# VectorE turns the expert rows, two more weight places in the second layer, and 16 KB pieces for the first layer's down weights, in a four-stage diffusion trunk on one core

## What is computed

```python
def hier_moe(x, w_group, b_group, w_router, b_router, w_gate, w_up, w_down):
    ...            # top-1 of 4 groups, then top-2 of its 4 experts, weights in `combine`
    y = jnp.zeros_like(x)
    for e in range(MOE_EXPERTS):                       # 16
        hdn = jax.nn.silu(x @ w_gate[e]) * (x @ w_up[e])     # 1024 -> 512
        y = y + combine[:, e:e + 1] * (hdn @ w_down[e])      # 512 -> 1024
    return y
```

## Time and profile before

| | us |
|---|---|
| time, three runs | 1120.63, 1123.94, 1128.57 |
| median | 1123.94 |
| profiled execution: time / its span | 1123.72 / 1121.9 |
| TensorE busy | 1031.8 (92%) |
| VectorE / ScalarE / GpSimd busy | 378.0 / 200.9 / 90.0 |
| granted TensorE clock, mean | 0.964 |

### The profile page before, as it was taken

The page is one execution under the profiler, slowest core; times in us unless marked ns, Lnnn a source line. Parts: engine busy times, 40 slices in busy tenths (PEclk is TensorE's granted clock), DMA queues, the critical chain, the costliest instruction groups (busy, mean ns, idle before and its releaser), DMA issues.

```text
span 1121.9 us, 20021 instructions
## 1 busy us (share of the span) xinstructions
PE 1031.8 (92%) x8395; PEld 623.4 (56%) x8395; DVE 378.0 (34%) x785; ACT 200.9 (18%) x383; POOL 90.0 (8%) x134
## 2 busy tenths in 40 slices
PE   2899999999997999999999976996897999998896
PEld 1343433448445788888888863543544655544442
DVE  1100799547546411111111104546516311111112
ACT  2200022325214200000000013314503100000001
POOL 4200000000100200000000014000010100000000
PEclk9799999998998999999999997997998899999998
DMA  9999868670021499999999994542022699999993
GB/s 341 397 394 387 316 218 293 249 299 2 4 76 75 141 397 393 419 388 384 411 381 405 415 370 128 214 150 75 1 78 113 252 407 413 398 400 399 416 427 143
DMA packets 71189, 313.31 MB, mean 279 GB/s; under 512 B 6280, under 2 KB 7912, under 8 KB 60641
## 3 DMA queue, kind: packets, MB, share of 16 engines
q1 hardware_dynamic: 58656, 283.64, 65.0%
q0 software_dynamic: 7168, 16.33, 4.4%
q10 hardware_dynamic: 5312, 12.59, 2.9%
HBM read 303.81 MB, written 15.20 MB: 284 GB/s over the span
## 4 chain that ended last, share of the span: by engine, by line
PE 78%; DMA 12%; DVE 5%; issue 2%; ACT 1%; SPq 1%; ACTq 0%; PEldq 0%; POOL 0%; POOLq 0%; DVEq 0%
PE ps L511 52%; PE ps L942 10%; DMA ring<-in_moe_w_gate 9%; PE ps L524 4%; PE ps L833 2%; PE ps L969 2%; DMA ring<-in_ada_w 2%; PE ps L931 2%; PE ps L1036 1%; SPq L450 1%; PE ps L767 1%; PE ps L955 1%; PE ps L1206 1%; DMA y_rows<-ar 1%; ACT hT L1295 0%
## 5 line engine op out<-in xcount | busy, mean ns | idle before, releaser
L511 PE MATMUL ps<-ring,ar 128*32 128x384 f32 (+5 forms) x3992 | 508.7, 471 | 16.6 <-DMA ring<-in_moe_w_gate 7.6
L511 PEld LDWEIGHTS ps<-ring,ar 128*32 128x32 f32 (+2 forms) x3992 | 216.7, 121 | 151.5 <-issue 84.1
L942 PE MATMUL ps<-ring,ar 128*32 128x128 f32 x1632 | 185.4, 274 | 0.0
L942 PEld LDWEIGHTS ps<-ring,ar 128*32 128x32 f32 x1632 | 177.6, 111 | 0.4
L511 PE MATMUL ps<-hT,ring 128*128 128x512 f32 x256 | 114.3, 601 | 0.1
L511 PE MATMUL ps<-ring,hT 128*128 128x512 f32 x192 | 87.1, 611 | 1.6 <-ACT hT L1295 1.6
L511 PEld LDWEIGHTS ps<-hT,ring 128*128 128x128 f32 x256 | 48.2, 192 | 64.2 <-issue 63.7
L2074 DVE SCALAR_TENSOR_TENSOR ar<-ar,cpar 128x512 f32<-128x512 f32 x120 | 79.6, 741 | 0.0
L1956 DVE COPY ar<-ps 128x384 f32<-128x384 f32 (+1 forms) x33 | 16.3, 493 | 181.5 <-PE ps L955 94.2
L524 PE MATMUL ps<-ring,silu_c 128*32 128x512 f32 x384 | 51.3, 655 | 22.0 <-DMA ring<-in_ada_w 22.0
L511 PEld LDWEIGHTS ps<-ring,hT 128*128 128x128 f32 x192 | 36.8, 195 | 49.7 <-issue 47.8
(11 more groups left out here) (321 smaller groups left out, 885.3 us busy)
## 6 DMA issues: line engine op xcount, KB each, us to landing
ring<-in_moe_w_gate SPq DMA_DIRECT2D x33, 2048.0 KB, 19.3
ring<-in_moe_w_up SPq DMA_DIRECT2D x33, 2048.0 KB, 18.8
ring<-in_moe_w_down SPq DMA_DIRECT2D x33, 2048.0 KB, 20.4
ring<-in_ada_w SPq DMA_DIRECT2D x24, 2048.0 KB, 13.5
ring<-in_even_w_in SPq DMA_DIRECT2D x5, 2048.0 KB, 18.9
ring<-in_odd_w_in SPq DMA_DIRECT2D x3, 2048.0 KB, 23.8
y_rows<-mla POOLq DMA_DIRECT2D x12, 384.0 KB, 11.4
y_rows<-ar ACTq DMA_DIRECT2D x16, 288.0 KB, 8.4
```

Source lines behind the costliest of these rows:

```text
L511: return nc.tensor.matmul(o, l, r, start=start, stop=stop)
L942: m = nc.tensor.matmul(ps[96:128, bank, g * P:(g + 1) * P], xgT[:, p, c, 32 * g:32 * g + 32], w[:, c, 3 * P:HID], start=c == 0 and g == 0, ...
```

## The change

Four things are changed together.

1. **Rows are turned by DVE.** `do_xt`, `do_hidden_t` and the copies from PSUM behind them go. DVE turns blocks of 32 by 32 elements from `xg` to `xgT` (`do_rows_turned`: 12 instructions of 32 partitions by 256 elements in layer 0, 8 in layer 1) and from `hid` to `hidT` (`do_hidden_t`: 16 instructions, of 96 elements in layer 0 and of 64 in layer 1). Only the first tile of each layer still goes through TensorE.
2. **Down weights of layer 0 in 16 KB pieces.** They are now loaded as in layer 1, row 4p+c. The hidden units must then stand in another order, so the gate and up products of layer 0 read their weight columns with a step: three of every four for the 384-column matmuls, and every fourth one (16 bytes apart) for the 128-column matmuls.
3. **Two more places in layer 1.** `x` and `hT` become one tensor `xh`, `gb` and `mla` one tensor `gm`, and two blocks of 16 KB per partition are cut from them (`beside`). Gate 15 and up 15 (`BESIDE`) are loaded there, before down 0; down 14 and down 15 take their places in `ring`.
4. **`final_norm_g`** goes to `gb[:, 0]` and is loaded after layer 1's gathers were issued, since its old place is one of the new weight places.

```diff
+BESIDE = (("g", 1, NEXP - 1), ("u", 1, NEXP - 1))
...
+    for n, (b, down) in enumerate(zip(BESIDE, (("d", 1, NEXP - 2), ("d", 1, NEXP - 1)))):
+        places[at[down]], turns[at[down]] = places[at[b]], turns[at[b]]
+        places[at[b]], turns[at[b]] = SLOTS + n, 2
...
             def expert_src(kind, l, e):
-                if kind == "d" and l == 0:
-                    return A["moe_w_down"][l, e, :, :].rearrange("(c p) n -> p c n", c=HC)
                 if kind == "d":
                     return A["moe_w_down"][l, e, :, :].rearrange("(p c) n -> p (c n)", c=HC)
...
+                    if l == 1 and b == ("d", 1, 0):
+                        for n, w in enumerate(BESIDE):
+                            if n == 0:
+                                sp.wait_ge(sem("block_used"), at["oin", 0, 1] + 1)
+                            else:
+                                sp.wait_ge(sem("q_rot"), 2)
+                            sp.dma_start(flat(at[w]), expert_src(*w)).then_inc(arrival(at[w]), 16)
+                    load(at[b], expert_src(*b), wide=flat(at[b]))
...
+                    wv = w[:, c, :].rearrange("p (i k) -> p i k", k=4)
                     if l == 0:
                         for g in range(3):
                             m = mm(ps[32 * g:32 * g + 32, bank, 0:3 * P], xgT[:, p, c, 32 * g:32 * g + 32],
-                                   w[:, c, 0:3 * P], c == 0, c == KC - 1)
+                                   wv[:, :, 0:3], c == 0, c == KC - 1)
                         for g in range(3):
                             m = nc.tensor.matmul(ps[96:128, bank, g * P:(g + 1) * P], xgT[:, p, c, 32 * g:32 * g + 32],
-                                                 w[:, c, 3 * P:HID], start=c == 0 and g == 0,
+                                                 wv[:, :, 3], start=c == 0 and g == 0,
...
+            def do_rows_turned(l, p):
+                for g in range(CAP[l] // 32):
+                    slots = slice(32 * g, 32 * g + 32)
+                    for q in range(4):
+                        m = V.transpose(xgT[32 * q:32 * q + 32, p, :, slots],
+                                        xg[slots, p, :].rearrange("s (c q i) -> s q c i", c=KC, q=4)[:, q, :, :])
+                return m
+
+            def do_hidden_t(l, p):
+                for r in range(4):
+                    cols = hid[32 * r:32 * r + 32, p, 0:hid_width(l)]\
+                        .rearrange("s (g q i) -> s q g i" if l == 0 and r == 3 else "s (q i c) -> s q c i", i=32, q=4)
+                    for q in range(4):
+                        m = V.transpose(hidT[32 * q:32 * q + 32, p, 0:3 - l, 32 * r:32 * r + 32], cols[:, q, :, :])
+                return m
...
                 def step(e, p, last=False):
                     hidden_t(l, e - 1, 1 - p)
                     if l == 1:
                         mix_weights(e - 1, 1 - p)
+                    if not last:
+                        rows_turned(l, e + 1, 1 - p)
                     hidden(l, e, p)
-                    if l == 0 and not last:
-                        xgt_half(e + 1, 1 - p)
                     y_half(l, e - 1, 1 - p)
...
             gathers(1)
+            pool.wait_ge(sem("x_added"), 2 * NT + 2 * NLAT)
+            pool.dma_start(gb[:, 0, :], A["final_norm_g"].rearrange("(a n) -> a n", a=1).to_broadcast([P, D]))\
+                .then_inc(sem("small_in"), 16)
             overflow(1)
```

More of the change, by code:

```diff
@@ L133, in ring_places @@
     after = range(len(freed), len(freed) + 3)
-    return [slot[b] for b in freed] + [k % SLOTS for k in after], [nth[b] for b in freed]
+    places, turns = [slot[b] for b in freed] + [k % SLOTS for k in after], [nth[b] for b in freed]
+    at = {b: k for k, b in enumerate(freed)}
+    for n, (b, down) in enumerate(zip(BESIDE, (("d", 1, NEXP - 2), ("d", 1, NEXP - 1)))):
+        places[at[down]], turns[at[down]] = places[at[b]], turns[at[b]]
+        places[at[b]], turns[at[b]] = SLOTS + n, 2
+    return places, turns
 def hybrid_dit(nc, A, out):
@@ L474, in moe_stream @@
                         overflow_stream(0)
-                    load(i, expert_src(kind, l, extra if e == LAST else e), wide=expert_dst(kind, l, SLOT[i]))
+                    k = at[BESIDE[e - NEXP + 2]] if l == 1 and kind == "d" and e >= NEXP - 2 else i
+                    load(i, expert_src(kind, l, extra if e == LAST else e), k, wide=flat(i))
             def overflow_stream(l):
@@ L604, in logits @@
                     m = nc.tensor.matmul(ps[32 * g:32 * g + 32, 0, j * P:(j + 1) * P], w_rt[:, 32 * c:32 * c + 32],
[L605 removed]
+                                         h_tail(l)[:, c, j * P:(j + 1) * P], start=c < 4, stop=c >= 4, skip_group_check=True)
                 m.then_inc(sem("logits_ps"), 1)
@@ L922, in rows_and_router @@
                     pe.wait_ge(sem("idx_ready"), 2)
-            def do_xt(l, p):
-                n = CAP[l]
-                for c in range(KC):
-                    bank, o = (3 + c // 4, (c % 4) * n) if l == 0 else (2, c * n)
-                    m = nc.tensor.transpose(ps[:, bank, o:o + n], xg[0:n, p, c * P:(c + 1) * P], ident[0:n, 0:n])
-                return m
             def do_product(l, p, up, w):
@@ L949, in do_product @@
                                wv[:, :, 2 * g:2 * g + 2], c == 0, c == KC - 1)
-                return m
-            def do_hidden_t(l, p):
-                if l == 0:
-                    for c in range(3):
-                        m = nc.tensor.transpose(ps[:, 2, c * P:(c + 1) * P], hid[:, p, c * P:(c + 1) * P], ident)
-                else:
-                    for c in range(2):
-                        m = nc.tensor.transpose(ps[:, 2, c * P:(c + 1) * P], hid[:, p, c:256:2], ident)
                 return m
@@ L1085, in experts, with step @@
                     key_spread()
-                def step(e, p, i, t, last=False):
+                def step(e, p, i, t):
                     gate_up(l, e, p, i, t, False)
@@ L1092, in step @@
                         mix_in(e - 2, p)
-                    hidden_t(l, e - 1, 1 - p)
                     gate_up(l, e, p, i + 1, t, True)
-                    if not last:
-                        xt(l, e + 1, 1 - p)
                     down(l, e - 1, 1 - p, i + 2, t)
@@ L1366, in experts, with step @@
             def experts(l):
-                xgt_half(l, 0, 0)
+                first_xgt(l)
                 silu(l, 0, 0)
-                xgt_half(l, 1, 1)
                 if l == 0:
                     last_taken()
-                def step(e, p, last=False):
+                def step(e, p):
                     silu(l, e, p)
-                    if not last:
-                        xgt_half(l, e + 1, 1 - p)
                     if l == 0:
@@ L1384, in experts @@
                 n = act.value_load(ov_n, min_val=0, max_val=MAXOV)
-                step(NEXP - 1, 1, last=l == 1)
+                step(NEXP - 1, 1)
                 overflow(l, n)
                 if l == 0:
-                    step(LAST, 0, last=True)
+                    step(LAST, 0)
                     A_(rstd[:, 15:16], eps, ACT.Sqrt)
@@ L2309, in gather @@
                     pool.wait_ge(sem("idx_ready"), 2)
-                if not (isinstance(e, int) and e < 2 and l == 0):
-                    pool.wait_ge(sem("xgT_ps"), EB[l] + e - 1)
+                if not (isinstance(e, int) and e < 2):
+                    pool.wait_ge(sem("xgT_dve"), EB[l] + e - 1 - l)
                 ex = e if isinstance(e, int) else bass.ds(e, 1)
```

162 lines of the change are left out of this document (74 added, 88 removed).

## The result

The changed kernel takes **1320.6 us** (median of 4 runs, 1310.7 to 1322.0) against 1122.6 us before (4 runs, 1120.6 to 1128.6): a ratio of 1.170, interval 1.166 to 1.175. It was forecast at 1117. The profiled execution spans 1318.8 us (1121.9 before). The clock is not the cause: over the span it was granted at 0.959 of full speed, and at 0.99 from 460 to 860 us.

A forecast was written before the change was run, and what follows sets the result against it. Layer 0 was taken as bound by TensorE, with weight loads nearly as slow, layer 1 by the DMA engines. Layer 0's 7.7 + 2.4 - 2 = 8.1 us less layer 1's 1.4 gave 6.7 us faster, 1117.0 us, range 1107 to 1127.

The forecast's parts named there:

- stepped columns: Rival: layer 0's fourth column group, reading every fourth element, slows gate and up 1.47 times; 59 us slower, 1183; chance 0.10.
- Turning on TensorE, layer 0: Layer 0: 1.29 us per expert leave TensorE, the stage becomes bound by the DMA engines; 7.7 us gained.
- the stock: Layer 0: weights loaded ahead of TensorE, run down to 5.9 us at gate 15; that much was to be gained.
- the pieces: Layer 0's down weights in 16 KB pieces: 0.15 us for each of 16 blocks, 2.4 us gained (0 to 21).
- list of signs: Expected profile: layer 0 periods 17.2 us at the start, some 17.7 from about the sixth expert, with waits for weights.
- The hand-over: From layer 0's end to layer 1: expert 15's store and the gather compete with more loads; 2 us lost (0 to 5.8).
- DVE: Both layers: transposes on DVE take 0.2 us each, hidden behind other work; cost nothing except in layer 1's tail.
- Two more places: Layer 1: they free TensorE only behind down 13's landing; 0.3 us gained, a loss of 3.3 at 0.425 per transpose.
- `final_norm_g` and the tail: Layer 1: 512 KB move into the bound stream, 1.7 us lost; with 0.3 gained by the places, 1.4 us later.
- Sum: Layer 0 8.1 us earlier, layer 1 1.4 later: 6.7 us faster than 1123.72, giving 1117.0 us.
- the gain is lost at the hand-over and in the tail: Rival: store and gather 5.8 us dearer, pieces worth nothing, transposes 0.4 us: 1127, or half, about 1121; chance 0.20.

The follow-up runs named there:

- d_step4_alone: The kernel before with one edit: the fourth column group reads every fourth column, transposes and pieces as before; 1330.1 us (one run).
- f_steps: The kernel before, with the fourth column group's 128 columns read in another step or pattern in each of 8 K steps; 1215.8 us (one run).
- a_dense16: The changed kernel with layer 0's gate and up on dense columns again, hidden rows turned by 12 VectorE instructions, not 16; 1126.1 us, ratio 1.0011.
- i_places_early: a_dense16 with the two more places holding layer 1's gate 2 and up 2 instead of gate 15 and up 15; 1122.4 us, ratio 0.9964.

## Why the prediction was wrong, step by step

**The step that failed is the price of the stepped columns.** The prediction named the rival with its mechanism and its point of decision (slower than before from a factor of 1.12 on), and then gave it a chance of 0.10 and a factor of 1.47, from weight loads at step two. Both were off. The factor is 2.2 (0.238 us per pass against 0.107), as d_step4_alone and f_steps show, and gate and up grew by 12.6 us per expert where 5.0 were priced. The argument against it was wrong in kind: "each fp32 column takes about 1.7 ns, a pace at which one element need not be slow to fetch". The pace of a pass is 0.83 ns per column (0.107 us over 128); a line of 16 bytes costs 1.9 ns (0.238 us over 128). The 1.7 was two passes taken as one: the row cited has 16 records for the 8 products of a down block, so it gives 0.89 ns per column and pass. The claim that one element need not be slow to fetch had no row behind it. The other fact held against it, that layer 1 reads two of four at almost full speed, was true (the row is gate 15's, not an up block's, with the same shape) and said nothing of one in four: two elements per line are the last cheap case (287 ns a record at step 2, 352 at step 3, 413 at step 4).

**What would have been the right weight.** The prediction itself said that one of four is in no row, and the nearest row it had, 206 ns against 140, pointed the right way, as the 413 ns against 279 now show. A term with no row of its own, on the engine that bounds the stage, multiplied by 17 experts, should not have had a chance of 0.10.

**Turning on TensorE, layer 0.** Judged by a_dense16. The stage does become bound by the DMA engines: TensorE waits there for up, gate and down blocks, 8.0 + 1.4 + 0.8 = 10.2 us in all, where it waited for none. At the hidden product of expert 15 a_dense16 is 8.7 us ahead (632.6 against 641.3 us, with first gate products 0.01 us apart); the forecast was 5.9 for the stock and 2.4 for the pieces. That is right, and so is the mechanism: the loads of gate blocks 3 to 15 landed 17.5 us apart (410.9 and 620.7), where 17.7 was forecast and 17.85 was before. The period at the start was 15.7 us (the loads of 393.68 and 409.36), as the prediction's own 15.9 said and not the 17.2 of its list of signs, and it held for eight experts, not five. What the prediction didn't follow is the expert in place 16. TensorE comes to its gate product 9.7 us ahead (642.57 against 652.26). Inside that product it stands still for 2.8 us, with the block landed at 637.2 and no releaser in the trace, and its granted clock is 0.53 from 641 to 652 us, against 0.84 from 651 to 662 before. At hidden product 16 5.1 us are left, and after the 5.1 us wait for VectorE 1.2 at down 16 (670.2 against 671.4). Why TensorE stands still there is not shown.

**The hand-over.** Forecast 2 us lost. The loads that follow the gathered rows are issued 4.3 us sooner (692.56 against 696.88 us), 0.8 less than the 5.1 at the result of down 15. Layer 1's first gate product keeps 2.9 (871.1 against 874.0). Forecast 8.1, so most of the miss without the stepped columns is here and in place 16.

**DVE.** Mis-sized: the turnings take 0.435 us (32 x 256), 0.39 to 0.41 (32 x 128), 0.29 (32 x 96) and 0.24 (32 x 64), not 0.2. VectorE's 17 us per expert were enough cover inside the stages, as forecast; at their ends there is none, and there the size counts, twice.

**Two more places.** Right in kind: down 13 starts 211.9 us behind layer 1's first gate product in a_dense16 and 212.7 before, and from it to the end 36.2 us against 35.2. So 0.8 is gained ahead of down 13 and 1.0 lost behind it, where the forecast was 0.3 gained there, and 3.3 lost at the dear end of a turning. i_places_early shows the reason given for it, that the places stand behind the last point at which the DMA engines bind: used early they are worth 5 to 8 us of layer 1 in the traces.

**`final_norm_g` and the tail.** Layer 1 with its end: forecast 1.4 us later, measured 0.2 (248.1 against 247.9), less than one execution can resolve. The row's own price, 1.7, was not measured alone.

**Sum.** Without the stepped columns the forecast was 6.7 us gained. The trace of a_dense16 has 2.7; its median lies between 2.4 us faster and 4.8 slower than before. So of the rest the rival "the gain is lost at the hand-over and in the tail" came nearest, with layer 0's last expert and the hand-over as its places and not layer 1's tail.

## What to carry to other kernels

A layout that makes one operand cheaper to load or to turn may be paid for by whoever reads it with a step, here with 12.6 us per expert: price the moving operand of TensorE first, per 16-byte line and not per element, and take 1.9 ns per line against 0.83 ns per fp32 column and pass, as worked out here from the K steps and from f_steps. Two fp32 elements of each line, read in order, cost little (an estimated 121 ns a pass against 109), and so do three of four (a record of 384 columns 501 ns against 490); one of each line more than doubled the pass (0.238 us against 0.107). Where turnings move to an engine with slack, look at the last round of each stage, where nothing covers them, and at what waits in front of them in that engine's queue; a buffer gained is worth what it brings forward in the bound queue, so the first blocks may repay it (5 to 8 us of layer 1 in single traces here) where the last did not.

## What the runs showed of the hardware that I had not expected

- TensorE's moving operand, fp32: in f_steps' rows but that of step 16 the pass is, by estimate and within 6 ns, the longer of 0.83 ns per column and 1.9 ns per 16-byte line read. Step 2 287 ns a record, step 3 352, steps 4, 5, 8 and 16 391 to 413, dense 273 to 279.
- Alignment alone did it: pairs inside a line 286 ns, the same pairs across a border 418.
- Two runs read in turn cost 304 ns, 31 above the cheapest; four cost 407, and the same four lines read again and again 399. It is as if two lines stayed at hand and a line to which the reading returns after three others were paid again; that is a reading of these times, not seen in a trace.
- An element read 128 times over cost what dense columns cost (273 ns against 273 to 279).
- With one of the four column groups slow, the others kept its pace: L535's records of 384 columns are hardly longer (501 ns against 490), but a K step starts 1.43 us after the last, not 0.64.
- VectorE turned 32 x 256 fp32 in 0.435 us and 32 x 64 in 0.236: by estimate about 0.17 us for each and 1 ns for each column. 32 x 128 with a source stepped by four took 0.39 to 0.41, more than the 0.30 of that line.
- The granted clock fell to 0.50 for some 7 us in one execution and not in another while TensorE was busy throughout: 0.77 on average from 140 to 155 us in seven traces, 1.00 in six, and the seven reach layer 0's first gate product 5 to 10 us later.
